# Squares, taps and gate rows regrouped among the engines of a four-layer mixer network

## The chip, the cores and the metric

One core of a Trainium2 chip runs the whole kernel. The metric is the device time of one launch in microseconds, as the median of several runs.

## What is computed

x is 512 tokens by 1024 features, in float32. Two layers of a first block are followed by two layers of a second one. Each layer normalises x, projects it, mixes over tokens, projects back and adds, then does the same with a gated feed-forward part.

```python
# block 1, per layer
proj = rms_norm(x, g) @ w_in                 # q 512, k 128, v 128, u 512, vv 512 columns
q, k = axial_rope(rms_norm per head of 64)   # 8 query heads, 2 key heads
attn = softmax(q k^T / 8) v
sg   = gelu(u) * (sg_w @ rms_norm(gelu(vv), per head of 64) + sg_b)
x += concat(rms_norm(attn), rms_norm(sg)) @ w_o ; x += silu(gate)*up @ w_down   (width-3 conv before)
# block 2, per layer
proj = rms_norm(x, g) @ w_in_2               # attention 3*256, conv 2*256, delta rule 3*512 + 512 gate + 8
dilated attention of 4 heads, with rotary(q), rotary(k)
y = causal_depthwise_conv(val * sigmoid(gate), dw)            # 31 taps, 256 channels
q, k, v = silu(causal conv of 4 taps); q, k = l2_normalize per head of 128
g = -exp(a_log) * softplus(a + dt_bias); beta = sigmoid(b)
decay[c, s] = exp(cumsum(g)[c] - cumsum(g)[s])                # chunks; then a triangular solve per head
```

## The kernel before, in words

Everything is kept transposed: features on the 128 partitions, the 512 tokens along the free dimension. One **unit** is one tile of 128 output features: `unit` (line 701) issues 24 matmuls of 128x128 by 128x512, because each float32 product over 8 tiles of features is made of three products of full-rate parts (fp32r): high weights by high h, high weights by low h, low weights by high h. The weights' parts are made while the kernel runs: SyncE loads `raw`, ScalarE copies it to `whi` (`hi_next`, line 1564), VectorE subtracts to get `wlo` (`low`, line 2276). There are two slots, so the parts for unit i+2 are made after unit i has ended, and `wlo` is asked for after 14 of the 24 matmuls. VectorE also takes each unit's result from PSUM (`acc_free`), two banks in turn.

The order on each engine is written out by hand, in loops over the units i; what stands in an iteration is done behind unit i, in program order, each engine on its own queue, with semaphores between them. No planner moves anything.

**Block 1's projection** has 14 units (v, k, four q, four vv, four u). For each of k, q and vv the squares (`qk_square`, `vv_square`, ScalarE) are summed over a head's 64 features by a matmul with a block matrix in plain float32, which the trace shows as two passes (`head_sums`, line 874, `gated_sums`, line 883), ScalarE makes the inverse root (`head_rs`), VectorE scales (`qk_norm`) and rotates (`qk_rotary`: product with the sine, shuffle, product with the cosine, difference; lines 2337 to 2343). GpSimd has almost nothing to do there.

**Block 2's projection** has 26 units. Units 0 to 3 are done together; 4 to 25 have, between them, the attention (rotary at i = 3 to 6 with GpSimd's partner products, line 660; scores, line 1127, with row maxima on VectorE, line 2666, before the next scores; `counted` on GpSimd, line 635), the short convolution of 4 taps (line 2687), the 31-tap convolution of two channel tiles on VectorE (`taps`, line 2710: 23 taps of both tiles in iterations 9 to 20, three of each tile in the first three), the squares of the delta rule's q and k for `l2_sums` (ScalarE line 1910, TensorE line 1176, float32), ScalarE's inverse roots `l2_rs` (lines 1568 and 1571), and in the last four iterations one head each: `head_in` makes two 128x512 matrices whose rows all hold the running sum of g and beta (lines 1197 and 1203, four float32 matmuls of 128 columns each), `head_scaled` on ScalarE reads them (lines 1930 to 1948).

**The level stage** follows: 24 steps of small matmuls (lines 1305, 1327, 1348) that invert the triangular matrices. ScalarE's copy to `xd` (line 2033) is read by the step two later. Beside it ScalarE makes the last eight taps' products for channel tile 1 (`tap_product`, line 2017) and GpSimd adds them (line 676); `mean_sum` (line 1358), at step 13, needs the last of them.

```python
for n in {16: (0, 1), 18: (2, 3), 19: (4, 5), 20: (6, 7)}.get(i, ()):
    l2_sums(n)                       # TensorE
for t in {17: (0, 1), 19: (2, 3), 20: (4, 5), 21: (6, 7)}.get(i, ()):
    l2_rs(t)                         # ScalarE
if n in (0, 1):
    tap_product(n)                   # ScalarE, level stage
if 2 <= n - 2 < CT - TAPS_IN:        # n >= 4
    act.wait_ge(late_tapped.sem, late_tapped.at(L, n - 4))
    tap_product(n - 2)
```

Of the kernel before, what the change touches and what calls it, by code (L numbers as in the profile page):

```python
# [6 lines left out]
P = 128  # L7
# [58 lines left out]
def network(nc, D, out, stop=None):  # L66
# [43 lines left out]
    TAPS_IN = sum(beside)  # L110
    N_IN2 = 3 * NA + 2 * NC + 4 * GH
# [15 lines left out]
    with ExitStack() as ctx:  # L127
# [19 lines left out]
        rstd = sb("rstd", [P, SEQ])  # L147
        ssq = sb("ssq", [P, SEQ])
# [26 lines left out]
        act_step, dve_step, pool_step = sem("act_step"), sem("dve_step"), sem("pool_step")  # L175
# [11 lines left out]
        vvsq_ready, vvstat_ready = sem("vvsq_ready", NS), sem("vvstat_ready", NS)  # L187
        vvrs_ready, vvn_ready = sem("vvrs_ready", NS), sem("vvn_ready", NS)
# [43 lines left out]
        beg_ready = sem("beg_ready")  # L232
        grow_ready, brow_ready, kT_ready, gvT_ready = (sem(n, GH) for n in ("grow_ready", "brow_ready", "kT_ready", "gvT_ready"))
# [5 lines left out]
        late_tapped, diag_kept = again(qkstat_ready, CT - TAPS_IN - 1), again(qkrs_ready, GH)  # L239
        tap_scaled = again(vvsq_ready, CT - TAPS_IN)  # L240
# [42 lines left out]
        with ExitStack() as on:  # L283
# [9 lines left out]
            kr = [sb("kr0", [P, SEQ], F32R, on=on)]  # L293
            vvT = sb("vvT", [P, TB, SGW], on=on)
# [9 lines left out]
            u = sb("u", [P, NS, SEQ], on=on)  # L304
            ao = sb("ao", [P, NQ, SEQ], on=on)
            rope = sb("rope", [P, 2, SEQ], on=on)
            perm = sb("perm", [P, P], on=on)
# [16 lines left out]
        with ExitStack() as on:  # L324
# [6 lines left out]
            with ExitStack() as early:  # L331
                zp = sb("zp", [P, 2, SEQ + GT - 1], on=early)
                cg = sb("cg", [P, NC, SEQ], on=early)
# [13 lines left out]
            perm2 = sb("perm2", [P, P], on=on)  # L347
# [15 lines left out]
        l2s = [cg[:, 0, :], cg[:, 1, :], za[:, 2 * NA, :], za[:, 2 * NA + 1, :], *(za[:, i, :] for i in range(2 * NA))]  # L363
        vns = tuple(t.rearrange("p (h d) -> p h d", d=P) for t in (ypad[:, 0, 0:GH * P], eg[:, 1, :]))
# [23 lines left out]
        def setup_tables():  # L388

            for dst, name in ((blk, "c_blk"), (perm, "c_perm")):  # L390
                yield dst[:], D[name]
            yield rope[:], D["c_rope"].rearrange("a p n -> p a n")
# [147 lines left out]
        def _(pool):  # L540
# [9 lines left out]
            for L in range(DEPTH):  # L550
# [25 lines left out]

                added_last = {4: (L, 3), 7: (L, NS + 1)}
# [16 lines left out]
            pool.dma_start(perm2[:], D["c_perm2"]).then_inc(c2_loaded.sem, 16)  # L594
# [31 lines left out]
            for L in range(DEPTH):  # L626
# [24 lines left out]
                def partners(i):  # L651

                    pool.wait_ge(acc_free.sem, (BASE2 + L * PAIRS2) * 2 + i + 3)
                    if i == 0:
                        pool.wait_ge(c2_loaded.sem, 3 * 16)
# [9 lines left out]
                for h in range(AH):  # L665
                    for kt in range(TB):
                        counted(h, kt)
# [4 lines left out]
                for n in range(CT - TAPS_IN):  # L672
                    pool.wait_ge(tap_scaled.sem, tap_scaled.at(L, n))
                    if n >= 1:
                        pool.wait_ge(late_tapped.sem, late_tapped.at(L, n - 1))
                    nc.gpsimd.tensor_tensor(yc[:, 1, :], yc[:, 1, :], kb[:, n % 2, :], ALU.add)\
                        .then_inc((late_tapped if n < CT - TAPS_IN - 1 else dw_ready).sem, 1)
# [13 lines left out]
            pool.wait_ge(c2_loaded.sem, 3 * 16)  # L691
# [3 lines left out]
        def _(pe):  # L695
# [164 lines left out]
            for L in range(DEPTH):  # L860
# [6 lines left out]
                def head_sums(i):  # L867

                    pe.wait_ge(qksq_ready.sem, qksq_ready.at(L, i))
                    if i == 0:  # L870
                        pe.wait_ge(rstd_ready.sem, rstd_ready.at(L * 2, 0))
                    if i >= 2:
                        pe.wait_ge(qkrs_ready.sem, qkrs_ready.at(L, i - 2))
# [2292 lines left out]
```

## Time and profile before

| | |
|---|---|
| time, median of 3 runs (lowest to highest) | 2551.18 us (2549.28 to 2551.55) |
| the profiled execution: its own time | 2552.15 us |
| the profiled execution: its span | 2550.4 us |
| mean granted TensorE clock | 0.995 of full speed |
| busy: PE, DVE, ACT, POOL | 2492.4, 1545.0, 1094.3, 227.2 us |
| chain of work that ended last | PE 88%, DVE 7%, ACT 2%, issue 1% |

PE is TensorE, DVE VectorE, ACT ScalarE, POOL GpSimd. A span is from the first to the last instruction; the execution's own time has 1.75 us around it. A busy share is an average over stages with different limits, so each stage is read by itself: the chain of waits says which engine's work the next step waited for.

### The profile page before, as it was taken

What the parts mean: (1) busy time and instruction counts of PE and PEld (TensorE: products, weight loads), DVE (VectorE), ACT (ScalarE), POOL (GpSimd) and SP (SyncE); (2) the same over time, 40 slices, a digit from 0 to 9 for tenths busy, and PEclk for the clock granted to TensorE, in tenths of its full rate; (3) what the DMA queues carried; (4) which work ended last, traced back from release to release, by engine and by line L of the source; (5) the groups of instructions that cost most, each with busy time, mean ns of one, the idle gap of its engine ahead of it and who ended that gap; (6) DMA issues with size and microseconds to landing.
All of it is one profiled execution on the core that took longest, in us unless ns stands there. A gap on an engine that the chain in (4) does not pass through costs nothing.

```text
span 2550.4 us, 36617 instructions
## 1 busy us (share of the span) xinstructions
PE 2492.4 (98%) x12846; PEld 1992.5 (78%) x12856; DVE 1545.0 (61%) x1994; ACT 1094.3 (43%) x1597; POOL 227.2 (9%) x186
## 2 busy tenths in 40 slices
PE   7999999999999999999999999999999999999998
PEld 5768888887668888887688778888776887788886
DVE  5766755757666736647986554344579865643444
ACT  4655423435554424433485442233334754431323
POOL 1010000000000000004212020000142120200000
PEclk9999999999999999999999999999999999999999
DMA  4203332333113333342120223233222202233333
GB/s 134 78 17 91 95 109 84 100 98 88 58 42 99 97 96 96 103 111 74 50 75 11 66 83 107 86 96 97 80 72 58 67 19 65 77 107 90 96 97 95
DMA packets 384483, 208.07 MB, mean 82 GB/s; under 512 B 9866, under 2 KB 380500, under 8 KB 384372
## 3 DMA queue, kind: packets, MB, share of 16 engines
q1 hardware_dynamic: 381284, 202.79, 27.5%
q0 software_dynamic: 2176, 3.06, 0.6%
q8 instruction: 65, 1.06, 0.2%
q10 hardware_dynamic: 912, 0.77, 0.1%
q14 instruction: 46, 0.38, 0.0%
HBM read 205.34 MB, written 2.10 MB: 81 GB/s over the span
## 4 chain that ended last, share of the span: by engine, by line
PE 88%; DVE 7%; ACT 2%; issue 1%; DMA 0%; POOL 0%; DVEq 0%; SPq 0%; ACTq 0%; POOLq 0%
PE ps L701 64%; PE ps L720 6%; PE ps L986 2%; DVE yc L2710 1%; DVE wlo L2276 1%; ACT whi L1564 1%; PE ps L1305 1%; PE ps L1164 1%; PE ps L1046 1%; PE ps L1048 1%; PE ps L1047 1%; PE ps L1176 1%; PE ps L1426 1%; PE ps L1428 1%; PE ps L1427 1%
## 5 line engine op out<-in xcount | busy, mean ns | idle before, releaser
L1564 ACT ACTIVATE whi<-raw 128x1024 fp32r<-128x1024 f32 (+1 forms) x354 | 395.8, 1118 | 989.4 <-PE ps L701 844.2
L701 PE MATMUL ps<-h_hi,whi 128*128 128x512 f32 x1920 | 761.8, 397 | 2.3 <-DVE za L2616 1.7
L701 PE MATMUL ps<-h_lo,whi 128*128 128x512 f32 x1920 | 750.0, 391 | 0.0
L701 PE MATMUL ps<-h_hi,wlo 128*128 128x512 f32 x1920 | 513.3, 389 | 0.0
L2276 DVE TENSOR_TENSOR wlo<-raw,whi 128x1024 fp32r<-128x1024 f32 (+1 forms) x354 | 467.0, 1320 | 64.2 <-ACT whi L1564 63.0
L701 PEld LDWEIGHTS ps<-h_hi,whi 128*128 128x128 f32 x1920 | 362.2, 189 | 84.3 <-issue 4.2
L701 PEld LDWEIGHTS ps<-h_lo,whi 128*128 128x128 f32 x1920 | 362.1, 189 | 78.7 <-issue 4.3
L701 PEld LDWEIGHTS ps<-h_hi,wlo 128*128 128x128 f32 x1920 | 360.5, 188 | 74.9
L701 PE MATMUL ps<-a_hi,whi 128*128 128x512 f32 x592 | 230.3, 389 | 0.0
L701 PE MATMUL ps<-a_lo,whi 128*128 128x512 f32 x592 | 230.3, 389 | 0.0
L3039 DVE TENSOR_TENSOR cv<-ps,rstd 128x512 f32<-128x512 f32 x80 | 55.3, 692 | 228.7 <-PE ps L701 228.7
L701 PE MATMUL ps<-a_hi,wlo 128*128 128x512 f32 x592 | 152.4, 389 | 0.0
L2525 DVE TENSOR_TENSOR pad<-ps,rstd 128x512 f32<-128x512 f32 x88 | 61.0, 693 | 130.6 <-PE ps L701 118.4
L701 PEld LDWEIGHTS ps<-a_lo,whi 128*128 128x128 f32 x592 | 111.1, 188 | 23.1
L701 PEld LDWEIGHTS ps<-a_hi,wlo 128*128 128x128 f32 x592 | 111.1, 188 | 23.0
L701 PEld LDWEIGHTS ps<-a_hi,whi 128*128 128x128 f32 x592 | 111.1, 188 | 23.0
L2488 DVE TENSOR_TENSOR x_sb<-x_sb,ps 128x512 f32 (+1 forms) x40 | 27.5, 687 | 110.1 <-PE ps L701 94.2
L2534 DVE SCALAR_TENSOR_TENSOR cv<-pad,pc,cv 128x512 f32<-128x512 f32 x88 | 66.1, 751 | 11.0
L1815 ACT ACTIVATE cv<-pad,pc,pb 128x512 f32<-128x512 f32 x88 | 70.6, 802 | 0.1
L2965 DVE COPY y_sb<-ps 128x512 f32<-128x512 f32 (+1 forms) x24 | 16.6, 691 | 88.8 <-PE ps L701 66.6
L1827 ACT ACTIVATE a_hi<-prod 128x512 f32 (+1 forms) x44 | 27.9, 633 | 97.8 <-DVE prod L2541 97.8
L2710 DVE SCALAR_TENSOR_TENSOR yc<-ypad,pd,yc 128x512 f32<-128x512 f32 x88 | 68.5, 819 | 1.6
(429 smaller groups left out, 3427.0 us busy)
## 6 DMA issues: line engine op xcount, KB each, us to landing
raw<-in_w_up SPq DMA_DIRECT2D x128, 512.0 KB, 3.8
raw<-in_w_down SPq DMA_DIRECT2D x64, 704.0 KB, 4.5
raw<-in_w_in SPq DMA_DIRECT2D x82, 512.0 KB, 3.8
raw<-in_w_gate SPq DMA_DIRECT2D x40, 512.0 KB, 3.8
raw<-in_w_o SPq DMA_DIRECT2D x16, 512.0 KB, 3.6
raw<-in_w_out SPq DMA_DIRECT2D x16, 512.0 KB, 3.7
xs<-in_x SPq DMA_DIRECT2D x2, 1024.0 KB, 6.8
raw<-in_w_gate SPq DMA_DIRECT2D x8, 256.0 KB, 2.8
```

What stands on the lines that cost most here:

```text
L701: return pe.matmul(ps[:, ACC[s], :], w[s][:, k, :], r[:, k, :], start=start, stop=stop)
L720: return pe.matmul(ps[:, ACC[s], :], w[s][:, k, :], r[:, k, :], start=start, stop=stop)
L986: pe.matmul(ps[:, TRN[h % 2], :], vaug[:, h // GROUP, h % 2, kt, :], probs[:, kt, :], start=(kt == 0), stop=(kt == TB - 1)).then_inc(PV_do ...
L1564: act.activation(whi[s][:, 0:kt, :], raw[s][:, 0:kt, :], ACT.Copy).then_inc(w_hi_ready.sem, 1)
L1815: act.activation(cv[s][:], pad[s][:, 1:SEQ + 1], ACT.Identity, scale=param(pb, L, 2 * NF + col), bias=param(pc, L, 2 * NF + col))\
L1827: act.activation(tile(a_hi, j), prod[:], ACT.Copy).then_inc(ahi_ready.sem, 1)
L2276: dve.tensor_tensor(wlo[s][:, 0:kt, :], raw[s][:, 0:kt, :], whi[s][:, 0:kt, :].bitcast(F32), ALU.subtract).then_inc(w_lo_ready.sem, 1)
L2488: dve.tensor_tensor(tile(x, n), tile(x, n), ps[:, ACC[s], :], ALU.add).then_inc(acc_free.sem, 1)
L2525: dve.tensor_tensor(pad[s][:, 1:SEQ + 1], ps[:, ACC[s], :], rstd[:], ALU.mult).then_inc(acc_free.sem, 1)
L2534: dve.scalar_tensor_tensor(cv[s][:], pad[s][:, 2:SEQ + 2], param(pc, L, col), cv[s][:], ALU.mult, ALU.add)\
L2710: ins = dve.scalar_tensor_tensor(yc[:, t, :], src, w, yc[:, t, :], ALU.mult, ALU.add)
L3039: dve.tensor_tensor(cv[s][:], ps[:, ACC[s], :], rstd[:], ALU.mult).then_inc(acc_free.sem, 1)
```

## The change

Block 1: the squares of k, q and vv are split by GpSimd into a full-rate high part and its remainder, and summed by two fp32r matmuls with an fp32r copy of the block matrix, in four banks in turn, one iteration later than before; the inverse root, norm, rotation and the parts of q move one iteration later too. GpSimd makes the rotation's product with the cosine. Block 2: the l2 squares are computed twice by ScalarE, once in float32, once rounded to fp32r; GpSimd subtracts; two fp32r matmuls sum. All of channel tile 1's 31 taps go to ScalarE (product) and GpSimd (sum): 20 of them beside units 10 to 21 (SIDE: two each for i = 10 to 17, one each for i = 18 to 21), eleven in the level stage, where GpSimd comes to them behind `delta_head(3)`. The running sums of g are taken at i = 12 instead of 20; g's sum and beta are split in two parts by VectorE (`decay_columns`, six small operations behind `low`), turned to rows once per layer, and each head then makes its two matrices with one fp32r matmul of 16 rows each. The last rotation of block 2 stands in front of its iteration's `low`.

```diff
+                def square_split(j):
...
+                    nc.gpsimd.tensor_copy(sq_hi[:, j % 4, :], square).then_inc(sq_split.sem, 1)
+                    pool.wait_ge(sq_split.sem, sq_split.at(L, 2 * j))
+                    nc.gpsimd.tensor_tensor(sq_lo[:, j % 4, :], square, sq_hi[:, j % 4, :].bitcast(F32), ALU.subtract).then_inc(sq_split.sem, 1)
+                def cosines(i):
...
+                    nc.gpsimd.tensor_tensor(probs[:, 2 + i % 2, :], zk[:] if i == 0 else zq[:, i - 1, :], rope[:, 0, :], ALU.mult)\
+                for j in range(NQ + 1):
+                    square_split(j)
+                    if j >= 2:
+                        cosines(j - 2)
...
+                    if h == 1:
+                        pool.wait_ge(qm_ready.sem, qm_ready.at(L, h))
+                        for j in range(NQ + 1, NQ + 1 + NS):
+                            square_split(j)
...
+                def side_tap(k):
+                    pool.wait_ge(tap_scaled.sem, tap_scaled.at(L, k))
+                    if k > 0:
+                        if k > 1:
+                            pool.wait_ge(late_tapped.sem, late_tapped.at(L, k - 2))
+                        nc.gpsimd.tensor_tensor(yc[:, 1, :], yc[:, 1, :], msq2[:, k % 2, :], ALU.add)\
+                            .then_inc((late_tapped if k < CT - 1 else dw_ready).sem, 1)
+                def l2_low(n):
+                    pool.wait_ge(l2sq.sem, l2sq.at(L, n))
+                    nc.gpsimd.tensor_tensor(l2_lo[n], l2s[n], qkr2[:, n % 4, :].bitcast(F32), ALU.subtract).then_inc(l2_split.sem, 1)
+                for i in range(10, 22):
+                    for n in {16: (0, 1), 17: (2, 3), 19: (4, 5), 20: (6, 7)}.get(i, ()):
+                        l2_low(n)
+                    p = i - 10
+                    if p < 2 * AH:
+                        for kt in range(2 * (p % 2), 2 * (p % 2) + 2):
+                            counted(p // 2, kt)
+                    for k in SIDE[i]:
+                        side_tap(k)
...
-                for n in range(CT - TAPS_IN):
+                for k in range(SIDE_IN, CT):
+                    side_tap(k)
...
-                    pe.matmul(ps[:, STAT[i % 2], :], blk[:], msq[:, i % 2, :], start=True, stop=True).then_inc(qkstat_ready.sem, 1)
+                    pe.matmul(bank, blk_r[:], sq_hi[:, j % 4, :], start=True, stop=False)
+                    pe.matmul(bank, blk_r[:], sq_lo[:, j % 4, :], start=False, stop=True)\
...
-                    if i - 2 <= NQ:
-                        head_sums(i - 2)
+                    if 0 <= i - 3 <= NQ:
+                        square_sums(i - 3)
...
-                    pe.matmul(ps[:, (STAT + ROT)[i % 4], :], ones[:], l2s[i], start=True, stop=True).then_inc(l2stat.sem, 1)
+                    pe.matmul(bank, negones[:], qkr2[:, i % 4, :], start=True, stop=False)
+                    pe.matmul(bank, negones[:], l2_lo[i], start=False, stop=True).then_inc(l2stat.sem, 1)
...
+                def turn_gate_parts():
+                    pe.wait_ge(gate_parts.sem, gate_parts.at(L, 0))
+                    for tb in range(TB):
+                        mm = pe.transpose(ps[0:4 * GH, TRN[1], tb * P:(tb + 1) * P], gate_split[:, tb, :].bitcast(F32), ident[:])
...
-                    for tb in range(TB):
-                        mm = pe.matmul(ps[:, ROT[0], tb * P:(tb + 1) * P], cols["g"][:, tb, h:h + 1].to_broadcast([P, P]),
-                                       tri[:], start=True, stop=True)
+                    pe.matmul(ps[:, ROT[0], :], gate_pick[0:n, h:h + 1].to_broadcast([n, P]), gate_rows[0:n, :],
+                              start=True, stop=True).then_inc(grow_ready.sem, 1)
...
+                    if kt == 0 and h == 1:
+                        pe.wait_ge(rows_kept.sem, rows_kept.at(L, 0))
...
-                    for n in {16: (0, 1), 18: (2, 3), 19: (4, 5), 20: (6, 7)}.get(i, ()):
+                    for n in {16: (0, 1), 18: (2, 3), 20: (4, 5), 21: (6, 7)}.get(i, ()):
...
+                def tap_product(k):
...
+                    if k >= 3:
+                        act.wait_ge(late_tapped.sem, late_tapped.at(L, k - 3))
...
-                    order.told(act.activation(l2s[i], gqkv[i], ACT.Square), l2sq, L, i)
+                    order.step(act.activation(l2s[i], gqkv[i], ACT.Square))
...
+                    order.told(act.activation(qkr2[:, i % 4, :], gqkv[i], ACT.Square), l2sq, L, i)
...
+                    for k in SIDE.get(i, ()):
+                        tap_product(k)
                     if i in (15, 18):
...
-                    if n in (0, 1):
-                        act.wait_ge(kk_ready.sem, kk_ready.at(L, GH - 2 + n))
-                        tap_product(n)
-                    if 2 <= n - 2 < CT - TAPS_IN:
-                        act.wait_ge(late_tapped.sem, late_tapped.at(L, n - 4))
-                        tap_product(n - 2)
+                    if n < CT - SIDE_IN:
+                        tap_product(SIDE_IN + n)
...
-                    order.step(dve.tensor_tensor(t1[:], z, rope[:, 0, :], ALU.mult))
-                    order.settle()
-                    order.told(dve.tensor_tensor(z, t1[:], t2[:], ALU.subtract), rope_ready, L, i)
+                    dve.wait_ge(cos_ready.sem, cos_ready.at(L, i))
+                    order.told(dve.tensor_tensor(z, probs[:, 2 + i % 2, :], t2[:], ALU.subtract), rope_ready, L, i)
...
-                        for t in range(NC):
+                        w, src = param(pd, L, D_DW + k * NC), ypad[:, 0, k:k + SEQ]
...
+                        if i == 2 * NA + 2:
+                            rotary(2 * NA - 1)
                         low(V + (i // 2 + 1), i % 2, KD)
+                    if i == 12:
+                        decay_columns()
+                    if i == 13:
+                        dve.wait_ge(gate_turned.sem, gate_turned.at(L, 0))
+                        order.told(dve.tensor_copy(gate_rows[0:4 * GH, :], ps[0:4 * GH, TRN[1], :]), rows_kept, L, 0)
```

Two tables (`perm`, `perm2`) that nothing reads are no longer loaded.

## Rows read from the trace of the kernel before

**Rows 1.** Chain of waits, block 1's projection, first layer: start us, us, what.
```profile
42.83 0.86 PE ps L874 x2
43.69 5.49 PE ps L701 x24
```
**Rows 2.** Timeline of VectorE there: start, us, what, [idle before].
```profile
70.18 0.68 DVE L2377 TENSOR_TENSOR vv<-ps,rstd 128x512 f32<-128x512 f32 x1
...
77.08 0.68 DVE L2377 TENSOR_TENSOR vv<-ps,rstd 128x512 f32<-128x512 f32 x1
```
**Rows 3.** Who TensorE waited for: us in total, times, longest.
```profile
PE ps L1127 <- DVE mx L2666: 5.9, 3, 2.8
...
PE ps L1127 <- ACT qkr L1961: 3.5, 2, 1.8
```
**Rows 4.** Chain of waits, block 2's projection, first layer: units 12, 13 and 14.
```profile
1221.12 7.29 PE ps L701 x24
...
1233.04 5.50 PE ps L701 x24
...
1241.49 5.55 PE ps L701 x24
```
**Rows 5.** Windows, units 12 to 14: busy us (x) by engine, PEclk, DMA share, GB/s.
```profile
1221.00:1258.00 37.00, 36.93 (x150) 26.57 (x150) 35.60 (x40) 10.65 (x19) 8.56 (x8) 0.95 0.16 43
```
**Rows 6.** Timeline of VectorE, units 11 to 14 of that projection.
```profile
1216.81 1.22 DVE L2666 TENSOR_REDUCE mx<-ps 128x2 f32<-128x1024 f32 x1
...
1227.84 1.22 DVE L2666 TENSOR_REDUCE mx<-ps 128x2 f32<-128x1024 f32 x1
...
1232.86 3.77 DVE L2687 SCALAR_TENSOR_TENSOR gq<-zp,pd,gq 128x512 f32<-128x512 f32 x3
...
1244.10 2.33 DVE L2687 SCALAR_TENSOR_TENSOR gq<-zp,pd,gq 128x512 f32<-128x512 f32 x3
```
**Rows 7.** Timeline of GpSimd, block 2's first layer.
```profile
1154.88 26.35 POOL L660 TENSOR_TENSOR probs<-za,rope 32x512 f32<-32x512 f32 x16 [14.91 <-DVE za L2616]
...
1233.59 2.49 POOL L635 TENSOR_TENSOR probs<-probs,times 128x512 f32<-128x512 f32 x2 [9.77 <-ACT probs L1892]
...
1357.13 11.43 POOL L676 TENSOR_TENSOR yc<-yc,kb 128x512 f32<-128x512 f32 x8
```
**Rows 8.** Timeline of ScalarE, from unit 15's end to the last inverse root.
```profile
1257.27 1.06 ACT L1564 ACTIVATE whi<-raw 128x1024 fp32r<-128x1024 f32 x1 [4.61 <-PE ps L701]
...
1276.29 1.06 ACT L1564 ACTIVATE whi<-raw 128x1024 fp32r<-128x1024 f32 x1 [3.65 <-PE ps L701]
...
1283.90 1.06 ACT L1564 ACTIVATE whi<-raw 128x1024 fp32r<-128x1024 f32 x1 [2.21 <-PE ps L701]
...
1291.82 2.62 ACT L1910 ACTIVATE za<-gk 128x512 f32<-128x512 f32 x4
...
1300.41 1.06 ACT L1564 ACTIVATE whi<-raw 128x1024 fp32r<-128x1024 f32 x1 [1.51 <-PE ps L701]
...
1308.06 1.06 ACT L1564 ACTIVATE whi<-raw 128x1024 fp32r<-128x1024 f32 x1 [1.19 <-PE ps L701]
...
1311.99 0.64 ACT L1571 ACTIVATE za<-lnt 128x512 f32<-128x512 f32 x1
```
**Rows 9.** Chain of waits, the l2 sums at unit 19 and the first head.
```profile
1293.13 1.72 PE ps L1176 x4
...
1313.40 0.89 PE ps L1197 x8
```
**Rows 10.** Timeline of ScalarE at the start of the level stage.
```profile
1350.96 1.41 ACT L2017 ACTIVATE kb<-ypad,pd 128x512 f32<-128x512 f32 x2
...
1356.31 0.39 ACT L2033 ACTIVATE gk<-ps 128x256 f32<-128x256 f32 x1 [1.64 <-PE ps L1348]
```
**Rows 11.** Chain of waits, the level stage's fifth step and the mean's sum.
```profile
1357.67 0.47 PE ps L1305 x16
...
1371.05 1.91 PE ps L1358 x4
```

More of the change, by code:

```diff
@@ L110, in network @@
     TAPS_IN = sum(beside)
+    SIDE = {**{10 + p: (2 * p, 2 * p + 1) for p in range(8)}, **{18 + n: (16 + n,) for n in range(4)}}
+    SIDE_IN = 20
     N_IN2 = 3 * NA + 2 * NC + 4 * GH
@@ L147, in network @@
         rstd = sb("rstd", [P, SEQ])
+        with ExitStack() as before_ssq:
+            gate_rows = before_ssq.enter_context(nc.sbuf_tensor("gate_rows", [P, SEQ], F32R))
         ssq = sb("ssq", [P, SEQ])
@@ L293, in network @@
             kr = [sb("kr0", [P, SEQ], F32R, on=on)]
+            with ExitStack() as before_vvT:
+                sq_lo = sb("sq_lo", [P, TB, SEQ], F32R, on=before_vvT)
             vvT = sb("vvT", [P, TB, SGW], on=on)
@@ L332, in network @@
                 zp = sb("zp", [P, 2, SEQ + GT - 1], on=early)
+                with ExitStack() as parts:
+                    cg_low = sb("cg_low", [P, NC, SEQ], F32R, on=parts)
+                    za_low = sb("za_low", [P, 3 * NA, SEQ], F32R, on=parts)
                 cg = sb("cg", [P, NC, SEQ], on=early)
@@ L2320, in _ @@
                     keep_rows(*ROW_TURNS[n - 4])
+            dve.wait_ge(setup_loaded.sem, SETUP)
+            order.step(dve.tensor_copy(blk_r[:], blk[:]))
             order.restart()
@@ L2597, in _ @@
                     low(V + 2, 0, KD)
+                    for n in range(2):
+                        of = [ident[:, (2 * n + e) * GH:(2 * n + e + 1) * GH] for e in range(2)]
+                        order.step(dve.tensor_tensor(gate_pick[:, n * GH:(n + 1) * GH], of[0], of[1], ALU.add))
                 dve.wait_ge(rstd_ready.sem, rstd_ready.at(G, 0))
@@ L2651, in gates, with decay_columns @@
                                                         expa[:].unsqueeze(1).to_broadcast([P, TB, GH]), ALU.mult, ALU.mult), g_ready, L, 0)
+                def decay_columns():
+                    dve.wait_ge(G_ready.sem, G_ready.at(L, 0))
+                    order.told(dve.tensor_copy(flat("gc"), ps[:, TRN[1], 0:NCOL]), gc_kept, L, 0)
+                    order.settle()
+                    order.told(dve.tensor_tensor(flat("dg"), ps[:, TRN[1], NCOL:2 * NCOL], flat("gc"), ALU.subtract), dg_ready, L, 0)
+                    for n, name in enumerate(("gc", "beta")):
+                        order.step(dve.tensor_copy(gate_split[:, :, 2 * n * GH:(2 * n + 1) * GH], cols[name][:]))
+                    order.settle()
+                    for n, name in enumerate(("gc", "beta")):
+                        hi, lo = (slice((2 * n + e) * GH, (2 * n + e + 1) * GH) for e in range(2))
+                        ins = dve.tensor_tensor(gate_split[:, :, lo], cols[name][:], gate_split[:, :, hi].bitcast(F32), ALU.subtract)
+                        if n == 0:
+                            order.step(ins)
+                        else:
+                            order.told(ins, gate_parts, L, 0)
                 def rotary(i):
```

179 lines of the change are left out of this document (92 added, 87 removed).

## The prediction, made before the changed kernel had run

> **What bounds the kernel now.** I began with the page: TensorE is busy for 2492.4 of 2550.4 us, 98% of the span, so every matmul taken out counts in full unless something else is late just there. So the chain of waits came next, stage by stage, and the timelines of the other engines beside it, to see how late each of them is already.
>
> In block 1's projection the chain is TensorE alone: 5.49 us of unit, then 0.86 us of float32 sum [rows 1]. VectorE takes 6.9 us from one unit's result to the next in one of its busiest iterations [rows 2], more than TensorE's 6.35, and is caught up only because lighter iterations follow.
>
> In block 2's projection TensorE waits for another engine twice a layer: 1.75 us for the last rotated tile and 2.83 us for a row maximum (1.8 and 2.8 are the longest [rows 3]). Unit 12, behind the longer of them, takes 7.29 us instead of 5.5 [rows 4]: in that stretch the granted clock is 0.95 of full speed in the mean, so 3.7 of 37 us were at 1.2 instead of 2.4 GHz [rows 5], right after TensorE had stood still. VectorE is busy for 35.6 of those 37 us; its row maxima come 11.0 us apart [rows 6]. From unit 15 on ScalarE is the late one: between 1257.27 and the last inverse root's end at 1312.63 it idles 3.65 + 2.21 + 1.51 + 1.19 = 8.6 us of 55.4 [rows 8], and TensorE's first head starts 0.8 us behind that root [rows 9].
>
> **The change, part by part.**
>
> Block 1's sums. A float32 sum of 512 columns takes 0.86 us [rows 1]. A full-rate matmul takes 5.49 / 24 = 0.23, two of them 0.46. Saved: 0.40 us, 18 times in two layers (k, four q, four vv): 7.2 us. GpSimd's split and cosine product (an estimate of 3.4 us a unit, from its 2.49 us for two such operations [rows 7] and a shorter copy) come one iteration earlier than TensorE and VectorE ask for them, so their latency is hidden by a 5.5 us unit. What they cost is on VectorE: beside GpSimd its operations with two SBUF inputs get longer. Three of them take 3.77 us beside 2.49 us of GpSimd and 2.33 alone [rows 6, 7]: 0.7 us for each GpSimd operation. Two such a unit cost 1.4 at most, the cosine product gives 0.7 back, and shifting qk_low apart from qk_norm evens the load. VectorE is then some 1 to 3 us behind in the last q iterations, about as much as `wlo`'s two slots bear. I take 0.5 us a layer for it, between 0 and 3. Block 1: -6.2. The rounded copy of the block matrix is one small copy on VectorE while it waits for the first inverse root, and two unread tables fewer are loaded: nothing, either way.
>
> Block 2, start. The last rotation no longer stands behind `low`, but its partner product ends on GpSimd only at 1181.23 [rows 7], so VectorE waits for it with `low` queued behind. Without a `low` of over 1.2 us in front the tile still comes early enough, and the 1.75 us wait goes; `wlo` is about 1 us later, and it has the first 14 matmuls of its unit, 3.2 us, as cover.
>
> Taps. VectorE does three fewer in each of iterations 9 to 11, then two, then one. In iterations 9 and 10 that is 5 or 6 times 0.78 (2.33 / 3 [rows 6]) less about 0.7 for GpSimd's first sum: 3.5 us off the way to the row maximum, more than the 2.83 us wait. But from iteration 11 on two sums by GpSimd cost VectorE about 1.4 and two taps fewer give 1.5, so its 11.0 us between maxima [rows 6] don't shrink, while TensorE, at full clock, would need about 10 (1221.12 to 1233.04 less the 1.8 of slow clock [rows 4]). Also new on VectorE: `decay_columns` (six tiny operations, an estimate of 1.2 us) at i = 12, for whose parts TensorE's four transposes wait (0.5 us, with some 0.45 of their own: half of an 0.89 us group of eight passes of that size [rows 9]), and the 0.7 us copy of the rows at i = 13, for which the attention's second head waits, with unit 15 behind it. I count VectorE's iteration 13 as 8.5 to 9.5 us against TensorE's 8.45 [rows 4]: a wait of 1.3, the 0.7 us copy and what precedes it. Together, with rotation, maximum and clock (1.8 us in unit 12, and some around it) on one side and these new waits on the other, unit 15 ends 3.5 us earlier per layer; bounds 0 and 8.
>
> Units 15 to 22. ScalarE gets ten products (0.7 each, from 1.41 for two [rows 10]) and eight more squares (2.62 / 4 = 0.65 each [rows 8]): 12.2 us into 8.6 us of idle. 1.1 of the rest is regained because its wait for VectorE in iteration 15 gets shorter. The last inverse root comes 2.5 us later after unit 15 than before; TensorE had 0.8 us of room [rows 9], so `grow` starts 1.8 us later, although TensorE's own work up to there has become shorter: three pairs of sums by 0.8 each and the running sums moved away. All of l2's 6.4 us in two layers (16 times 0.40) is lost in this wait. **Late next** is ScalarE's silu of v with its table load, then `head_scaled` of head 0.
>
> Heads. A group of 0.89 us for g [rows 9] and one of the same shapes for beta become two matmuls of 0.23: 1.3 us a head. The first two heads are held by ScalarE, so I count half of 4 x 1.3, 2.5 us. From unit 15 to the level stage: +1.8 - 2.5 = -0.7 a layer. Bounds: -6 (no wait at ScalarE) and +4 (its wait brings the clock down again, as in [rows 4, 5]).
>
> Level stage. GpSimd starts its sums behind `delta_head(3)`, at 1357.13, and needs 1.43 us each [rows 7]: eight end at 1368.56, 2.5 us before the mean is asked for [rows 11]; eleven take 4.3 us more. And ScalarE's product 22 at step 2 waits for the sum of 20, so that its copy for step 1 (1356.31 [rows 10]) comes at about 1359.2, where step 5 had begun at 1357.67 [rows 11]: +1.9 us a layer, and it covers the mean's wait. Bounds 0 and 3.5.
>
> **Sum.** -6.2 + 2 x (-3.5 - 0.7 + 1.9) = -10.8 us. The profiled execution took 2552.15 us itself, so 2541.3; it lies 0.97 us above the median of the runs, so 2540.4, and I say 2540.
>
> One rule speaks against the change. The rows show 0.7 us of VectorE for each GpSimd operation beside it [rows 6, 7]. The Trainium skill, page "SBUF — State Buffer", section "SBUF: two separate sides", says that the pair of ports which the two engines share is an exclusive lock, held for the whole instruction, while the other fully blocks. By that rule a sum would cost its whole length; it is the second rival. That two operations together cost 1.44 us beside 2.49 speaks for a shorter hold than the whole instruction.
>
> **The rivals.**
>
> *All of the matrix work lands.* ScalarE's products fit in after all. Then 34 x 0.40 + 8 x 1.3 - 0.9 for the transposes, with 2 x (1.75 + 2.83) of waits and 5 us of slow clock, give 37 us: 2514. For it: TensorE's 98%. Against it: 12.2 us of work in 8.6 us of idle. Two thirds of it, where some waits behind ScalarE stay, is 2526.
>
> *VectorE becomes the bound through GpSimd* (the slower side). Place: iterations 10 to 16, where it has no idle time. Fifteen GpSimd operations stand there a layer that were not there before (thirteen sums, two l2 differences); at their whole length, 2.49 / 2 = 1.25 us [rows 7], instead of 0.7 that is 8.2 us a layer, and in block 1 the 6.2 us shrink to some 2. It gives -10.8 + 16.4 + 4 = +9.6: 2561. It decides from a cost of about 1.0 us per GpSimd operation. For it: VectorE's full timeline there; against it: 0.7 in the rows.
>
> *The new waits bring the clock down.* Two waits of 2 to 4 us a layer, behind ScalarE at head 0 and in the level stage, each followed by slow matmuls as unit 12 was: +2.1 each, its 1.8 and a little around it [rows 4]. It gives -10.8 + 8.4 = -2.4: 2549. For it: both are as long as the two that TensorE has now; against it: not every such stop need bring it.
>
> **How the numbers follow.** The forecast has 0.5, the first rival 0.22 (most of it at its milder value), the second 0.12, the third 0.16. Faster than 0.2% (5.1 us, about what a measurement of this kernel can tell from no change) are nearly all of the forecast, the first rival and a small part of the third: 0.73. Within 0.2%: most of the third, a little of the forecast and the second: 0.16. Slower: 0.11. The forecast's own bounds reach from 2524 to 2552 when its terms go together. The range goes from 2518, which takes in the milder first rival, to 2553, which leaves out most of the second rival.
>
> **What would show it.** Right: no wait of line 1127 for the rotated tile or the maximum, and few slow-clock stretches there; ScalarE without idle time from unit 15 to head 0; TensorE waiting for the last inverse root, 3 to 4 us; ScalarE's copies in the level stage at the pace of GpSimd's sums; VectorE's two-input operations at up to 1.6 us beside them. Wrong in the steps: idle time on ScalarE at units 18 to 21, a level stage no longer than before, or a VectorE iteration well below 9 us at units 12 and 13. The whole would be wrong if `wlo` were late in block 1 (units longer than 5.49 us there), or if the first rival's sum came out.

## The result, and the profile after

The changed kernel takes 2568.46 us (median; 2567.32 to 2569.53) against 2551.32 (2549.28 to 2551.55) for the kernel before, run beside it: a ratio of 1.0068, 95% interval 1.0054 to 1.0083. It is 17 us slower. I had said 2540, with 2518 to 2553 as the range.

Set against the trace before, stretch by stretch: the same unit or step starts some us later or earlier than before, and the table has what each stretch adds to that. Block 1 is taken to the first unit behind its attention.

| stretch | predicted per layer | first layer | second layer |
|---|---|---|---|
| block 1 | -3.1 | +1.8 | 0.0 |
| block 2, to unit 15 | -3.5 | -2.6 | -2.7 |
| unit 15 to the level stage | -0.7 | +6.4 | +7.4 |
| level stage, to the mean's sum | +1.9 | +2.8 | +2.8 |

The sum is +15.9 where -10.8 was predicted. Two terms carry 23.2 of the 26.7 us of error: the stretch from unit 15 to the level stage (15.2) and block 1 (8.0).

Page of the changed kernel: busy time by engine, and the chain by engine.

```profile
PE 2483.8 (97%) x12742; PEld 1986.1 (77%) x12752; DVE 1557.5 (61%) x1951; ACT 1130.7 (44%) x1659; POOL 386.5 (15%) x291
...
PE 79%; DVE 10%; ACT 5%; issue 3%; POOL 3%; DMA 0%; DVEq 0%; SPq 0%; ACTq 0%; POOLq 0%
```

TensorE is busy for 8.6 us less than before, so matrix work did go; GpSimd has 159 us more. The chain, 88% TensorE before, now runs through the other engines. Who TensorE waited for (us in total, times, longest), where [rows 3] stood:

```profile
PE ps L765 <- DVE wlo L2352: 8.2, 4, 3.6
...
PE ps L1267 <- ACT za L1640: 6.4, 2, 3.3
PE ps L1254 <- DVE gate_split L2744: 4.5, 2, 2.3
PE ps L1374 <- ACT gk L2113: 3.8, 2, 1.9
...
PE ps L940 <- POOL sq_lo L604: 3.7, 2, 1.8
...
PE ps L765 <- ACT whi L1633: 2.5, 3, 1.0
...
PE ps L1225 <- DVE gate_rows L2939: 1.9, 1, 1.9
PE ps L957 <- ACT wT L1742: 1.8, 2, 0.9
```

The row maximum's and the rotated tile's long waits are gone, as predicted. New are late low parts of the weights (8.2), the last inverse root (6.4), the split gate columns (4.5), the level stage's copy (3.8) and, in block 1, GpSimd's split (3.7).

The costliest is the wait for unit 21's low part. ScalarE, iteration 18 and the two behind it (start, us, what, idle before):

```profile
1293.37 0.64 ACT L1988 ACTIVATE za<-gk 128x512 f32<-128x512 f32 x1
1293.91 0.62 ACT L1993 ACTIVATE qkr<-gk 128x512 fp32r<-128x512 f32 x1
...
1298.00 1.04 ACT L1633 ACTIVATE whi<-raw 128x1024 fp32r<-128x1024 f32 x1
1298.95 0.71 ACT L2039 ACTIVATE gv<-zp,pd 128x512 f32<-128x512 f32 x1
...
1308.11 0.72 ACT L2039 ACTIVATE gv<-zp,pd 128x512 f32<-128x512 f32 x1 [4.01 <-DVE zp L2696]
```

VectorE there, behind three rows of iteration 11 that answer to [rows 6]:

```profile
1213.51 1.21 DVE L2763 TENSOR_REDUCE mx<-ps 128x2 f32<-128x1024 f32 x1
...
1218.71 3.52 DVE L2784 SCALAR_TENSOR_TENSOR gq<-zp,pd,gq 128x512 f32<-128x512 f32 x3
1222.15 2.29 DVE L2352 TENSOR_TENSOR wlo<-raw,whi 128x1024 fp32r<-128x1024 f32 x1
...
1299.69 4.19 DVE L2784 SCALAR_TENSOR_TENSOR gv<-zp,pd,gv 128x512 f32<-128x512 f32 x3 [5.28 <-ACT gv L2039]
1303.80 2.28 DVE L2352 TENSOR_TENSOR wlo<-raw,whi 128x1024 fp32r<-128x1024 f32 x1
```

GpSimd, as [rows 7]:

```profile
1212.47 2.26 POOL L719 TENSOR_TENSOR yc<-yc,sqt 128x512 f32<-128x512 f32 x1
...
1219.94 3.42 POOL L719 TENSOR_TENSOR yc<-yc,sqt 128x512 f32<-128x512 f32 x2
...
1301.60 3.40 POOL L725 TENSOR_TENSOR za_low<-za,qkr 128x512 fp32r<-128x512 f32 x2
...
1362.71 16.14 POOL L719 TENSOR_TENSOR yc<-yc,sqt 128x512 f32<-128x512 f32 x11
```

TensorE, timeline of the same stretch:

```profile
1306.13 2.41 PE L765 MATMUL ps<-h_hi,wlo 128*128 128x512 f32 x7 [3.57 <-DVE wlo L2352]
...
1314.25 1.75 PE L765 MATMUL ps<-h_hi,wlo 128*128 128x512 f32 x7
...
1319.85 0.50 PE L1267 MATMUL ps<-gate_rows,gate_pick 16*128 16x512 f32 x1 [3.18 <-ACT za L1640]
```

Read them together. ScalarE squares each of four tiles twice (1293.37 to 1298.0), and only behind that come the next high part and the short convolution's centre. VectorE has idled 5.28 us for that centre. Then three taps and a low part take 4.19 + 2.28 us beside GpSimd, where they take 2.33 + 1.22 alone. TensorE, out of high-part work, stands for 3.57 us, and then makes seven matmuls in 2.41 us that take 1.75 otherwise. VectorE takes that late unit's result late, and so ScalarE in its turn idles 4.01 us for VectorE before it can go on towards the last inverse root. Windows of that stretch (us, then busy us of PE, PEld, DVE, ACT, POOL, then PEclk, DMA share, GB/s), after:

```profile
1293.00:1326.00 33.00, 24.54 (x95) 19.04 (x94) 25.62 (x29) 27.12 (x42) 9.84 (x7) 0.90 0.23 64
```

and before:

```profile
1293.00:1326.00 33.00, 33.00 (x175) 27.26 (x174) 28.36 (x41) 28.84 (x57) 0.00 (x0) 1.00 0.23 65
```

TensorE worked 24.5 of 33 us instead of all of them, and a mean clock of 0.90 says that 6.6 of the 33 us were at 1.2 instead of 2.4 GHz.

Chain of waits further on, answering to [rows 4, 11]:

```profile
1240.70 5.55 PE ps L765 x24
...
1365.15 1.01 PE ps L1374 x16
1366.16 0.85 PE ps L1396 x16
...
1379.46 1.91 PE ps L1427 x4
```

Unit 14 starts 0.8 us earlier than before (1241.49). The level stage's fifth step comes 7.5 us later, the next steps take 0.85 instead of 0.47, and the mean comes 8.4 later.

### The profile page after: what moved, and what is told of

Its sections match the earlier page's. It is cut to its first block, busy times and chain, and to the rows that moved or that the text cites. A ratio compares the mean times of both kernels' runs of the same rounds, so it can differ in the third digit from the quotient of the medians.

```text
span 2565.9 us, 36614 instructions
## 1 busy us (share of the span) xinstructions
PE 2483.8 (97%) x12742; PEld 1986.1 (77%) x12752; DVE 1557.5 (61%) x1951; ACT 1130.7 (44%) x1659; POOL 386.5 (15%) x291
## 4 chain that ended last, share of the span: by engine, by line
PE 79%; DVE 10%; ACT 5%; issue 3%; POOL 3%; DMA 0%; DVEq 0%; SPq 0%; ACTq 0%; POOLq 0%
PE ps L765 58%; PE ps L784 6%; POOL probs L708 2%; PE ps L1045 1%; DVE wlo L2352 1%; DVE gq L2784 1%; DVE yc L2805 1%; DVE gv L2784 1%; ACT whi L1633 1%; PE ps L1105 1%; PE ps L1374 1%; PE ps L1107 1%; PE ps L1106 1%; DVE gk L2784 1%; PE ps L1497 1%
## 5 line engine op out<-in xcount | busy, mean ns | idle before, releaser
L2352 DVE TENSOR_TENSOR wlo<-raw,whi 128x1024 fp32r<-128x1024 f32 (+1 forms) x354 | 483.6, 1367 | 61.0 <-ACT whi L1633 59.8
L719 POOL TENSOR_TENSOR yc<-yc,sqt 128x512 f32<-128x512 f32 x60 | 90.5, 1508 | 33.2 <-ACT sqt L1969 28.3
L650 POOL TENSOR_TENSOR h_lo<-pad,h_hi 128x512 fp32r<-128x512 f32 x9 | 14.6, 1621 | 476.8 <-ACT h_hi L2248 476.8
```

The source lines that it names most:

```text
L719: nc.gpsimd.tensor_tensor(yc[:, 1, :], yc[:, 1, :], msq2[:, k % 2, :], ALU.add)\
L2352: dve.tensor_tensor(wlo[s][:, 0:kt, :], raw[s][:, 0:kt, :], whi[s][:, 0:kt, :].bitcast(F32), ALU.subtract).then_inc(w_lo_ready.sem, 1)
```

## The experiments

The experiments came in five groups. The variants of a group were timed beside the kernel before on one chip, so differences are taken to that group's own median of the kernel before (2551.10, 2551.07, 2551.05, 2550.69, 2550.99 us). From the runs' spread, a difference between two variants is uncertain by an estimated 1 to 3 us.

**First group: the parts.** My theory by then: the matrix time is saved, and new waits, made by ScalarE's and GpSimd's extra work, eat it. `e1_block1` is the kernel before with all edits of block 1; `e2_block2` has all the others; `e3_taps_back` is the changed kernel without this part (as in the kernel before):

```diff
-                    for k in SIDE[i]:
-                        side_tap(k)
...
-                    for k in SIDE.get(i, ()):
-                        tap_product(k)
...
```

and `e5_rows_rot` the kernel before with only `decay_columns`, `turn_gate_parts`, the running sums at i = 12, the new `head_in` and the rotation in front of `low`.

> The kernel before with block 1's part of the change alone: squares split by GpSimd, full-rate sums, everything behind them one iteration later, the cosine product on GpSimd. Theory (new waits): the 7.2 us of matmul time are given back by waits that the new order makes (the key copies and the wT copy in one ScalarE iteration, the first gated sum behind GpSimd's split, a late low part) and by slow clock behind them. In the trace of the changed kernel the first scores come 2.2 us later than before in layer 0 and about 0.4 us later per layer 1, so 2551.3 + 2.4 = about 2554. Rival (the prediction's term): matmul time saved less 0.5 us a layer of VectorE contention, 2545.

> The changed kernel with block 1 as before, so block 2's part alone. Theory (new waits): block 2 carries nearly all of the loss; its own shifts in the changed kernel's trace are +8.0 in its first layer and +9 in its second up to the chunk stage's end, less the +0.4 it starts with: 2551.3 + 15 = about 2566. Rival (the two parts hurt each other, through the clock or through weights that arrive late from block 1): clearly less than 2566, 2556 or below, and the two parts alone do not add up to the whole 17 us.

> The changed kernel with channel tile 1's taps as before: 23 of them on VectorE beside the units, eight on ScalarE and GpSimd in the level stage. Squares, l2 parts and the gates' rows stay changed. Theory (the taps are the cause): ScalarE loses ten products and GpSimd thirteen sums beside the units, so the late low part in front of unit 23 (3.6 us), the wait for the last inverse root (3.2 us), the level stage's wait (1.9 us) and their slow clock go, and the row maximum's wait (2.8 us, with slow unit 12) comes back: about 2551.3 + 2.4 - 2 x 1.75 - 2 x 3 (heads) = 2544, between 2538 and 2550. Rival (the doubled l2 squares on ScalarE are the cause): the waits in front of unit 23 and of head 0 stay, and it is 2558 or more.

> The kernel before with only two parts of the change: the gates' sums turned to rows once a layer (with the running sums at unit 12), and the last rotation in front of the weights' low half. Nothing is added on ScalarE or GpSimd. Theory: both land, 2 x 1.75 for the rotation and 2 x 4 x 1.3 for the heads, less 2 x 0.9 for the transposes and up to 2 x 1.5 for the wait on the two gate parts: 2551.3 - 3.5 - 10.4 + 1.8 + 3 = about 2542. Rival (ScalarE and VectorE set the pace of the heads, and the row maximum's wait grows by what the rotation gives): within 3 us of 2551.

Measured: 2553.35 (ratio 1.0007, 0.9998 to 1.0017), 2569.56 (1.0071, 1.0054 to 1.0088), 2556.65 (1.0021, 1.0012 to 1.0031) and 2547.04 (0.9985, 0.9976 to 0.9995). Block 1's part gives no gain; block 2's alone costs all of the loss. e3 came 13 us above what I expected and just short of the rival's 2558: the l2 part costs by itself, about 7 us (5.5 - 2.3 + 4.1). Rows and rotation gain, but 4 us where I expected 9.

**Second group: which engine.** Theory A: a GpSimd operation beside VectorE's is what costs. Theory B: ScalarE's queue. `f1_taps` is block 2's part without the l2 edits. `f2_sums_short` makes the 19 sums a layer beside the units on one column, `f3_both_short` ScalarE's products too; `f4_diff_short` starts from e3, makes the l2 differences on one column and lets both matmuls read the high part. In the last three a part of the convolution or of the l2 sums is left out.

```diff
+                    w = 1 if k < SIDE_IN else SEQ
...
-                        nc.gpsimd.tensor_tensor(yc[:, 1, :], yc[:, 1, :], msq2[:, k % 2, :], ALU.add)\
+                        nc.gpsimd.tensor_tensor(yc[:, 1, 0:w], yc[:, 1, 0:w], msq2[:, k % 2, 0:w], ALU.add)\
...
-                    nc.gpsimd.tensor_tensor(l2_lo[n], l2s[n], qkr2[:, n % 4, :].bitcast(F32), ALU.subtract)
+                    nc.gpsimd.tensor_tensor(l2_lo[n][:, 0:1], l2s[n][:, 0:1], qkr2[:, n % 4, 0:1].bitcast(F32), ALU.subtract)
```

> Block 2's part without the two-part l2 sums (these stay one float32 square and one float32 sum), block 1 as before: so the gates' rows, the rotation and all of tile 1's taps on ScalarE and GpSimd. The runs so far give, if parts add, -4.1 for rows and rotation and 18.5 - 7.4 + 4.1 for the taps: 2551.1 + 11 = 2562, between 2558 and 2566. If ScalarE's queue is what hurts (taps and squares together fill it), it is clearly less than the sum, 2556 or below, since without the eight extra squares the products have room.

> As the run with the taps alone, but GpSimd's twenty sums beside the units are made on one column instead of 512 (so tile 1's convolution is left out for the most part); ScalarE's products and the eleven sums of the level stage stay. Theory A (GpSimd beside VectorE is the cost: VectorE's two-input operations get longer and its low parts late): most of the loss up to the level stage goes, 10 us or more less than the run with the taps alone, 2551 or below. Theory B (ScalarE's queue is the cost): at most 3 us less.

> As the run before, and ScalarE's nineteen products beside the units on one column too. What VectorE gained by having fewer taps stays, and the eleven products and sums of the level stage. Theory A: little below the run with short sums alone, by 3 us or less, so about 2548. Theory B: here the loss goes, 8 us or more below it. In both the level stage keeps its +2.8 us a layer.

> The changed kernel with the taps as before (the run of 2556.6), with GpSimd's eight l2 differences a layer on one column and the second matmul reading the high part once more (so the sums are wrong in size by a factor near two). ScalarE's doubled squares and both matmuls stay. Theory A (GpSimd's operations lengthen VectorE's): half or more of the 7.4 us that the two-part l2 sums cost goes, 2552 or below. Theory B (ScalarE's eight extra squares stand in front of the next weights' high part and of the short convolution's centre): it stays, 2555 or more.

Measured: 2554.95, 2539.13, 2537.15 and 2553.86. With the taps alone theory A stands: the sums (38 in two layers, since tap 0 needs none) cost 15.8 us of the launch, 0.42 each; ScalarE's 38 products cost 2.0. By the start of the units in both traces, 6.0 and 5.0 us of it (first and second layer) are lost before unit 15. VectorE's iteration 11, without the sums (f2, VectorE):

```profile
1216.26 2.60 DVE L2740 SCALAR_TENSOR_TENSOR gq<-zp,pd,gq 128x512 f32<-128x512 f32 x3
1218.78 1.22 DVE L2309 TENSOR_TENSOR wlo<-raw,whi 128x1024 fp32r<-128x1024 f32 x1
```

and with them (f1, VectorE, then GpSimd):

```profile
1216.09 3.52 DVE L2739 SCALAR_TENSOR_TENSOR gq<-zp,pd,gq 128x512 f32<-128x512 f32 x3
1219.53 2.29 DVE L2308 TENSOR_TENSOR wlo<-raw,whi 128x1024 fp32r<-128x1024 f32 x1
```

```profile
1217.32 3.42 POOL L681 TENSOR_TENSOR yc<-yc,sqt 128x512 f32<-128x512 f32 x2
```

5.81 against 3.82 us: two sums cost VectorE 1.0 us each. For l2 the differences are only 2.8 of some 7 us, between what the two theories had said; that the rest is ScalarE's squares is likely, but not shown. f1 stayed 7 us under the additive guess, so l2 and taps cost more together than by themselves. The traces show where: from unit 15 to unit 25 rows and rotation alone (e5) give 2.2 us in each layer. With the taps added (f1) the stretch is 0.4 and 1.1 us longer than before, with l2 added (e3) 2.0 and 1.7, with both (the changed kernel) 6.7 and 7.7. Against e5 the taps cost some 3 us there, l2 some 4, and both together 9 to 10, 2 to 3 us more than their sum.

**Third group: mending.** `g1_b1_fixed` moves, in block 1, the copies of the turned spatial weights in front of the square and three gated sums one iteration on; `g2_b1_cos_dve` takes the cosine products back to VectorE as well. `h2_rows_even_b1` adds g1's block 1, with the cosine products on GpSimd, to `h1_rows_even`, which is e5 with one edit:

```diff
-    beside = [3, 3, 3, 2, 2, 2, 2, 2, 1, 1, 1, 1]
+    beside = [2, 2, 2, 2, 2, 2, 2, 2, 2, 2, 2, 1]
```

> Block 1's part alone (the run of 2553.4) with two orders mended: ScalarE's copies of the turned spatial weights stand in front of its square in iteration 5, and of the gated sums only the first is made at unit 10, the other three (and their inverse roots) one iteration later. Theory (order): the 7.2 us of matmul time are real, and two waits and what they trigger ate them: 0.9 us behind the key copies, 1.8 us for GpSimd's split of the second gated square, a slow unit behind it. With both gone about 2.5 us a layer stay: 2546. Rival (contention: VectorE beside GpSimd is the limit anyway): the waits move to the weights' low parts, and it stays at 2551 or more.

> As the run before, and the product with the cosine back on VectorE, ahead of the difference, so GpSimd has only the splits. The cosine product on GpSimd saves VectorE 0.75 us, and costs it about 1.0 us if one GpSimd operation of 512 columns holds VectorE's two-input operations up by that much, as the runs on the taps show. Contention theory: the same or up to 2 us faster than with the cosines on GpSimd. Rival (GpSimd's help is worth its price): 1 to 3 us slower.

> Rows and rotation alone (the run of 2547.0), and the 23 tap pairs on VectorE spread evenly: 2 in each of iterations 9 to 19 and one in 20, instead of 3, 3, 3, 2, 2, 2, 2, 2, 1, 1, 1, 1. No work goes to another engine. Theory (VectorE is the limit in iterations 9 to 13 and has room later): each of the three pairs taken out of iterations 9 to 11 gives 1.4 us on the way to the row maximum (2.8 us) and to the gates' rows (1.4 us), so both waits and the slow unit behind the first go: 2 x 4 us less, 2539. Rival (ScalarE and VectorE are just as late in iterations 17 to 20): 2545 or more.

> The run before with block 1's part in the mended order. If parts add and the mended block 1 gives 2.5 us a layer: 2534. If block 1 stays where it was, 2541.

Measured: 2550.92 (0.9997, 0.9988 to 1.0007), 2549.91 (0.9996, 0.9987 to 1.0006), 2539.11 (0.9953, 0.9937 to 0.9970) and 2538.82 (0.9952, 0.9936 to 0.9969). The even spread does what I expected. The mended order of block 1 gives 2.4 us back where I expected seven, hardly more than the runs' spread, and nothing can be measured on top of h1; where the cosine products stand makes no difference that these runs can tell.

**Fourth group: l2, spread and place.** `i1_even` is the kernel before with the `beside` edit alone. `i4_l2_on_even` is h1 with the l2 part; `i3_l2_one_square` the same with the float32 squares and the differences on one column and both matmuls reading the rounded squares, which leaves the low part out. `h3_rows_late` is h1 with the gates' columns and rows later, on TensorE and VectorE alike (they then use another PSUM bank, and it is the first head that waits for the rows):

```diff
-                    if i == 12:
+                    if i == 20:
                         decay_columns()
-                    if i == 13:
+                    if i == 21:
                         dve.wait_ge(gate_turned.sem, gate_turned.at(L, 0))
...
```

> The kernel before with one edit: the 23 tap pairs on VectorE spread evenly over iterations 9 to 20. Theory (VectorE's own load ahead of the row maximum is the wait): the 2.8 us wait and the slow unit behind it go in both layers, 2551.1 - 2 x 4.5 = about 2542, and the rows and rotation are worth only the rest, 3 us, of the run of 2539.1. Rival (the spread helps only once the rotation is moved): 2548 or more.

> Rows, rotation and even taps (the run of 2539.1) with the l2 sums as two full-rate matmuls, but both of the same high part: ScalarE's float32 squares and GpSimd's differences are made on one column, so that the engines beside TensorE have no more work than before, and the sums are wrong in size. Theory (the matmul time is real, the extra work on the other engines eats it): up to 2 x 8 x 0.40 = 6.4 us less where no wait takes its place, 2534, between 2532 and 2537. Rival (the last inverse root sets head 0's start whatever TensorE saves): 2538 or more.

> Rows, rotation and even taps with the l2 part as the change has it: squares twice on ScalarE, differences on GpSimd. By the sum of the earlier runs it costs 7.4 us: 2546.5. Theory (ScalarE's order: four extra squares in each of iterations 15 and 18 stand in front of the next high part, and of the short convolution's centre that VectorE waits for): 2543 to 2549. Rival (the 7.4 came from VectorE being late already in front of it, which the even taps have mended): 2540 or less.

> The run of 2539.1 with the gates' running sums, their split columns and the copy of the turned rows at iterations 20 and 21 instead of 12 and 13, where VectorE is late. Theory (place, not work): the waits of 1.5 us for the rows and 0.9 us for the split columns go, twice: 2534.5. Rival (VectorE is as late at 20 and 21, now that taps stand there): the waits reappear in front of head 0 and it stays at 2538 or more.

Measured: 2542.39 (0.9967, 0.9954 to 0.9979), 2539.48, 2550.54 (0.9998, 0.9989 to 1.0008) and 2535.71 (0.9939, 0.9923 to 0.9956). The spread alone is worth 8.3 us. The matmul time of l2 is worth nothing even when it comes free (2539.5 against 2539.1; I had expected 2534), and the extra squares and differences cost 11.1 us, 1.5 us beyond my range for i4. Who TensorE waited for in the first block 2 layer, i3:

```profile
PE ps L1225 <- ACT za L1598: 2.4, 1, 2.4
```

and i4:

```profile
PE ps L1225 <- ACT za L1598: 3.1, 1, 3.1
PE ps L718 <- DVE wlo L2309: 2.1, 2, 1.8
```

So what TensorE saves in the sums it stands waiting for the last inverse root. (i3 and i4, like the change, also have the last four sums one unit later. In i3's trace ScalarE never idles for a sum between units 19 and 22, so that place is not what holds the root back.) VectorE in i4, four taps without GpSimd beside them and four with its differences, then GpSimd:

```profile
1281.88 2.87 DVE L2763 SCALAR_TENSOR_TENSOR yc<-ypad,pd,yc 128x512 f32<-128x512 f32 x4
...
1289.53 5.84 DVE L2763 SCALAR_TENSOR_TENSOR yc<-ypad,pd,yc 128x512 f32<-128x512 f32 x4
```

```profile
1290.09 6.44 POOL L676 TENSOR_TENSOR za_low<-za,qkr 128x512 fp32r<-128x512 f32 x4 [13.08 <-ACT qkr L1943]
```

h3, 3.0 us better than h1, shows that the place of the gates' work was a cost: h1's waits in the first layer were

```profile
PE ps L1176 <- DVE gate_rows L2886: 1.5, 1, 1.5
...
PE ps L1203 <- DVE gate_split L2686: 0.9, 1, 0.9
```

and h3 has neither.

**Fifth group: block 1's last question.** `j1_b1_no_split` is g2 with ScalarE writing rounded squares that both matmuls read, and on GpSimd two copies of one column in place of the copy and the subtraction, so the low part of the squares is left out. `h4_late_b1` is h3 with g1's block 1.

> Block 1's part in the mended order, cosines on VectorE, and GpSimd's splits on one column: ScalarE rounds its squares itself and both matmuls read them (so the means are wrong in size). Beside VectorE nothing is left on GpSimd. Contention theory: of the 7.2 us of matmul time 5 or more land, 2546 or below. Rival (the order of the steps, moved one iteration later, is the limit): 2549 or more, with the same waits of TensorE as in the runs with the split.

> The kernel of 2535.7 (rows late, rotation, even taps) with block 1's part in the mended order. By the two earlier pairs (2551.1 to 2550.9 alone, 2539.1 to 2538.8 on top of the even taps) it gives 0.2 to 0.3 us: 2535.5, no difference that can be measured. If clock windows in block 1 spoiled those, up to 3 us less: 2533.

Measured: 2543.27 (0.9972, 0.9961 to 0.9983) and 2534.05 (0.9936, 0.9923 to 0.9950). Without GpSimd's splits 7.7 us come off, all of the 7.2 us of matmul time; with them 6.6 us are given back (g2), 0.37 us for each of 18 splits. Not all of that is VectorE's: in the two layers of g2 TensorE waits 2.2 us for a split itself, and 3.7 us for low parts in the units where j1 has 0.6. Waits in block 1's first projection and start of attention, g2:

```profile
PE ps L726 <- DVE wlo L2292: 1.8, 1, 1.8
...
PE ps L901 <- POOL sq_lo L593: 1.1, 1, 1.1
```

and j1:

```profile
PE ps L725 <- DVE wlo L2291: 0.3, 1, 0.3
```

One operation of VectorE in g2, the rotation's difference, alone and beside a split, then that split:

```profile
78.60 0.69 DVE L2361 TENSOR_TENSOR zq<-t 128x512 f32<-128x512 f32 x1
...
85.90 1.67 DVE L2361 TENSOR_TENSOR zq<-t 128x512 f32<-128x512 f32 x1
```

```profile
85.40 1.62 POOL L593 TENSOR_TENSOR sq_lo<-sqt,sq_hi 128x512 fp32r<-128x512 f32 x1
```

h4 is the best version found: 17 us below the kernel before, 34 below the changed one, though 2 us below h3 is within the spread. Its windows of units 10 to 15 and of the stretch shown above:

```profile
1205.00:1262.00 57.00, 56.49 (x233) 39.93 (x235) 54.77 (x64) 24.47 (x41) 13.83 (x12) 1.00 0.21 56
1293.00:1326.00 33.00, 31.82 (x177) 25.49 (x176) 29.56 (x47) 28.35 (x65) 3.87 (x3) 1.00 0.26 76
```

## Why the prediction was wrong

Two steps failed. The larger is the term for units 15 to 22 (15.2 us of the error, with the heads' term), the other the price of a GpSimd operation, with its latency taken as hidden, which is most of block 1's 8.0 us.

- *"0.7 us for each GpSimd operation".* It came from one pair of operations [rows 6, 7], and I carried it to others. The sums cost VectorE 1.0 us each (f1 against f2), a split's subtraction 0.98 (0.69 to 1.67), four taps beside the l2 differences 2.97 us more. The pair in the rows multiplies by `times`, a bfloat16 tile, where the others have float32 operands alone; whether that made it cheaper, no run separates. 1.0 is the point that I had named for the second rival, *VectorE becomes the bound through GpSimd*, at 0.12. Its mechanism is what f1 against f2 shows in the taps, and a part of block 1's loss. Its size is not: it put 8.2 us a layer on iterations 10 to 16, and the changed kernel missed the forecast by only 0.8 to 0.9 us a layer up to unit 15. Its 2561 was 7 us short, since it had kept the forecast's term for l2.
- *Block 1, -6.2.* The 7.2 us of matmul are real (j1: -7.7). I charged 0.5 us a layer for VectorE; the splits cost 3.3 a layer (j1 to g2), the order of the new steps perhaps 1.2 a layer more (e1 to g1, hardly more than the spread). "About as much as `wlo`'s two slots bear" was argued from a mean; a 1.8 us wait for a low part was there (g2; 0.3 in j1). And that GpSimd's latency is hidden by a 5.5 us unit is false for the second gated square, which ScalarE makes late: TensorE waits 1.8 us for its split in the changed kernel, and 1.1 us even in the mended order.
- *Until unit 15, -3.5 a layer.* Measured -2.6 and -2.7. Rotation and row maximum went as said; the wait for the gates' parts, put at 1.3, was 2.3 with a stretch of slow clock.
- *Units 15 to 22: all of l2's 6.4 us lost in the wait for the last inverse root, and otherwise 1.8 us later.* The first half held (i3: no gain). The second is the step that failed most. I set 12.2 us of new ScalarE work against 8.6 us of idle and asked only when the last inverse root comes. (The trace has 11.0 us of idle there: 1.75, 0.28 and 0.38 us had been left out. So there was more room, not less. And 2.5 less 0.8 is 1.7, half of 5.2 is 2.6; neither matters.) The squares stand in one block in front of the next high part and the short convolution's centre, so the lateness reaches VectorE and, through unit 21's low part, TensorE before the root is asked for: 3.57 us and a slow clock, and GpSimd's sums and differences make VectorE's late work longer still. Then ScalarE idles 4.01 us for VectorE at unit 21, which was my own sign of a wrong step ("idle time on ScalarE at units 18 to 21"). The stretch came out at +6.4 and +7.4 instead of -0.7; neither part alone does that (f1, e3), the two together do. The bound that I gave, +4, was too small for the same reason. How this cost divides between squares and differences is not settled: the differences were 2.8 of some 7 us on e3; the rest of i4's 11.1 us was not divided, and no run has the squares in another place.
- *Heads, -2.5 a layer.* On top of the even spread, rows and rotation are worth 3.6 us (i1 to h1), another 3.0 once the gates' work stands where VectorE has room. These 6.6 us stand against 8.5 in my terms (2 x 1.75 and 2 x 2.5), so the size was about right only in the last form.
- *Level stage, +1.9.* The mechanism was right: ScalarE's product waits for GpSimd's sum behind `delta_head(3)`, its copy behind that, TensorE 1.9 us. Measured +2.8, since the following steps ran at the slow clock (0.85 instead of 0.47 each).
- *The third rival, clock.* It was there too: 0.90 in the mean of the 33 us above, right behind the 3.57 us wait. But it follows the waits: h4, without them, has 1.00 in the same stretch.

What I missed altogether was in the trace of before: VectorE was the late engine in iterations 9 to 13 and idle by 2.97 us or so at unit 19. One list of numbers moves its work there and gives 8.3 us, more than any edit of the change.

## What to carry to other kernels

Work given to GpSimd is not off VectorE's books: price it on VectorE wherever that engine runs operations with two inputs from SBUF (here about 1.0 us of 1.3, where one pair had shown 0.7), and give it only what saves VectorE more than that, or where VectorE has idle time. Before matrix work is removed, ask which engine TensorE would then wait for; and when a step's total fits into an engine's idle time, look at what stands behind it in that queue. First spread the work that an engine already has over its own idle time; it puts nothing on the others.

## What the runs showed of the hardware

The contention goes both ways, and depends on VectorE's operands. GpSimd's subtraction takes 1.62 us beside VectorE (1.30 alone, as the first split in g2), and even copies of one column on GpSimd, in j1:

```profile
89.80 1.06 POOL L592 CAST sq_lo<-sq_hi 128x1 fp32r<-128x1 f32 x1
90.92 0.18 POOL L590 CAST sq_lo<-sq_hi 128x1 fp32r<-128x1 f32 x1
```

take 1.06 us when they fall into VectorE's 1.25 us low part, 0.18 otherwise. VectorE's reduction out of PSUM kept its 1.21 us beside a 2.26 us GpSimd sum (1213.51 and 1212.47 above), so such work pays nothing. That fits the rule of the Trainium skill that I had doubted (page "SBUF — State Buffer", section "SBUF: two separate sides"): the shared pair of ports is an exclusive lock for the whole instruction. Here a GpSimd operation of 1.3 us cost about 1.0 us, most of its length but not all, and one of the pair in [rows 7] 0.7.
